# Differential attention's projections: query and value slabs alternate, in place of all queries ahead of all values

## The reference

```python
q, k, v = jnp.split(h @ w_in, 3, axis=-1)                    # latent tokens; the context gives k and v alone
q = rms_norm(q.reshape(b, l, DIFF_HEADS, 2, DIFF_HEAD_DIM), q_gain)
k = rms_norm(k.reshape(b, l, DIFF_HEADS, 2, DIFF_HEAD_DIM), k_gain)
q_l = apply_rope(q_l, cos, sin)
k_l = apply_rope(k_l, cos, sin)
```

## Time and profile before

| | us |
|---|---|
| median of 3 runs | 1271.04 (1270.48 to 1272.4) |
| the profiled execution | 1273.77 |
| its span in the profile | 1272.1 |
| q0 to q7 and the units just behind them, 565 to 613 in the span | 48 |
| the other value units, 613 to 647 | 34 |

### The profile page before, as it was taken

The page is one execution under the profiler, slowest core; times in us unless marked ns, Lnnn a source line. Parts: engine busy times, 40 slices in busy tenths (PEclk is TensorE's granted clock), DMA queues, the critical chain, the costliest instruction groups (busy, mean ns, idle before and its releaser), DMA issues.

```text
span 1272.1 us, 18656 instructions
## 1 busy us (share of the span) xinstructions
PE 1195.5 (94%) x7112; PEld 987.8 (78%) x7112; DVE 703.3 (55%) x1170; ACT 544.3 (43%) x1002; POOL 86.2 (7%) x124
## 2 busy tenths in 40 slices
PE   7999999999999998898978899999989788999998
PEld 4665787787788886677955899999979775798467
DVE  3544567676533334779369554445574635455843
ACT  3234321222232223555258554445465556466742
POOL 0002011122100002000000200000000000020500
PEclk9999999999999999899999999999999999999899
DMA  8889355687522232224320345655534332374011
GB/s 304 315 299 323 130 180 164 196 284 248 189 96 100 100 99 66 66 67 133 100 67 1 100 159 174 194 177 188 160 119 145 100 100 66 61 225 138 33 47 53
DMA packets 121366, 183.32 MB, mean 144 GB/s; under 512 B 4305, under 2 KB 92672, under 8 KB 121296
## 3 DMA queue, kind: packets, MB, share of 16 engines
q1 hardware_dynamic: 113744, 154.64, 36.8%
q0 software_dynamic: 7552, 27.73, 6.9%
HBM read 181.31 MB, written 1.05 MB: 143 GB/s over the span
## 4 chain that ended last, share of the span: by engine, by line
PE 80%; DVE 10%; ACT 4%; issue 3%; POOL 1%; DMA 1%; DVEq 0%; SPq 0%; ACTq 0%; POOLq 0%
PE ps L458 19%; PE ps L459 19%; PE ps L460 19%; PE ps L774 2%; PE ps L775 2%; PE ps L776 2%; PE ps L814 2%; DVE wl L443 1%; PE ps L2038 1%; PE ps L2082 1%; ACT wh L436 1%; DVE big L885 1%; PE ps L2369 1%; PE ps L2371 1%; PE ps L2370 1%
## 5 line engine op out<-in xcount | busy, mean ns | idle before, releaser
L443 DVE TENSOR_TENSOR wl<-raw,wh 128x1024 fp32r<-128x1024 f32 (+1 forms) x246 | 296.4, 1209 | 263.3 <-ACT wh L436 260.7
L458 PE MATMUL ps<-hh,wh 128*128 128x256 f32 (+2 forms) x1256 | 420.3, 335 | 17.9 <-DVE hl L588 11.4
L459 PE MATMUL ps<-hl,wh 128*128 128x256 f32 (+2 forms) x1256 | 411.2, 327 | 0.0
L460 PE MATMUL ps<-hh,wl 128*128 128x256 f32 (+2 forms) x1256 | 410.2, 327 | 0.0
L436 ACT ACTIVATE wh<-raw 128x1024 fp32r<-128x1024 f32 (+1 forms) x246 | 252.8, 1031 | 278.1 <-PE ps L460 256.3
L458 PEld LDWEIGHTS ps<-hh,wh 128*128 128x128 f32 x1256 | 238.8, 190 | 60.6 <-issue 27.5
L460 PEld LDWEIGHTS ps<-hh,wl 128*128 128x128 f32 x1256 | 239.2, 190 | 20.9
L459 PEld LDWEIGHTS ps<-hl,wh 128*128 128x128 f32 x1256 | 238.1, 190 | 22.3 <-issue 1.9
L458 PE MATMUL ps<-ah,wh 128*128 128x256 f32 (+2 forms) x392 | 132.5, 338 | 7.4 <-DVE big L870 3.7
L459 PE MATMUL ps<-al,wh 128*128 128x256 f32 (+2 forms) x392 | 129.7, 331 | 0.0
L460 PE MATMUL ps<-ah,wl 128*128 128x256 f32 (+2 forms) x392 | 129.5, 330 | 0.0
(11 more groups left out here) (225 smaller groups left out, 1427.1 us busy)
## 6 DMA issues: line engine op xcount, KB each, us to landing
raw<-in_ffn_w_in SPq DMA_DIRECT2D x44, 1024.0 KB, 5.1
raw<-in_ffn_w_out SPq DMA_DIRECT2D x22, 1024.0 KB, 5.0
raw<-in_w_in SPq DMA_DIRECT2D x22, 1024.0 KB, 5.3
big<-in_w_ada SPq DMA_DIRECT2D x16, 1024.0 KB, 9.3
big<-in_w_ada POOLq DMA_DIRECT2D x24, 512.0 KB, 4.5
ex<-in_w_ada POOLq DMA_DIRECT2D x24, 512.0 KB, 5.2
raw<-in_diff_w_in SPq DMA_DIRECT2D x12, 1024.0 KB, 5.1
raw<-in_w_out SPq DMA_DIRECT2D x8, 1024.0 KB, 4.9
```

The source lines that it names most:

```text
L443: ins = nc.vector.tensor_tensor(place(wl), v, place(wh).bitcast(F32), ALU.subtract)
L458: nc.tensor.matmul(o, w_hi, m_hi, start=first, stop=False, **kw)
L459: nc.tensor.matmul(o, w_hi, m_lo, start=False, stop=False, **kw)
L460: return nc.tensor.matmul(o, w_lo, m_hi, start=False, stop=last, **kw)
```

## The change

In `slab_starts` the stages `diff_q` and `diff_v` (four slabs each) become one stage `diff_qv` of eight slabs, which alternate: query slab s stands at `DQ_G[s]`, value slab s at `DV_G[s]` behind it. The unit list is built in that order, and SP loads the slabs in it. The list is now k0 to k7, q0 q1, v0 to v3, q2 q3, v4 to v7, q4 q5, v8 to v11, q6 q7, v12 to v15. The number and the size of all instructions and transfers are the same.

```diff
@@ -132,7 +132,7 @@
-              ("diff_k", 4), ("diff_q", 4), ("diff_v", 4), ("diff_out", 4), ("ffn1_in", 22), ("ffn1_out", 11),
+              ("diff_k", 4), ("diff_qv", 8), ("diff_out", 4), ("ffn1_in", 22), ("ffn1_out", 11),
@@ -145,6 +145,8 @@
+DQ_G = [G["diff_qv"] + 2 * s for s in range(4)]
+DV_G = [G["diff_qv"] + 2 * s + 1 for s in range(4)]
@@ -643,13 +645,13 @@
-        for h in range(8):
-            DIFF_UNITS.append(unit("head", 2 * G["diff_q"] + h, KD, 0, P, L, 1,
-                                   red="half", dim=64, gain="dq", rope=("cos_d", "sin_d", L), out=[],
-                                   dst=dq[:, h, :]))
         for s in range(4):
+            for h in (2 * s, 2 * s + 1):
+                DIFF_UNITS.append(unit("head", 2 * DQ_G[s] + h % 2, KD, 0, P, L, 1,
+                                       red="half", dim=64, gain="dq", rope=("cos_d", "sin_d", L), out=[],
+                                       dst=dq[:, h, :]))
             for t in range(4):
-                DIFF_UNITS.append(unit("token", 2 * (G["diff_v"] + s) + 1, KD, 0, 256, P, 2 * (t == 3), tok=t * P,
+                DIFF_UNITS.append(unit("token", 2 * DV_G[s] + 1, KD, 0, 256, P, 2 * (t == 3), tok=t * P,
                                        dst=dv[:, t, s * 256:(s + 1) * 256]))
@@ -1415,9 +1417,9 @@
-            for g, col in ((G["diff_k"], D), (G["diff_q"], 0), (G["diff_v"], 2 * D)):
-                for s in range(4):
-                    load(g + s, d["diff_w_in"][0, :, col + s * 256:col + (s + 1) * 256], KD, 256)
+            for g, col, s in [(G["diff_k"] + s, D, s) for s in range(4)] + \
+                    [(g, col, s) for s in range(4) for g, col in ((DQ_G[s], 0), (DV_G[s], 2 * D))]:
+                load(g, d["diff_w_in"][0, :, col + s * 256:col + (s + 1) * 256], KD, 256)
```

## The result

| | before | after |
|---|---|---|
| median of the runs, us | 1271.52 (6 runs, 1270.48 to 1274.2) | 1266.42 (6 runs, 1264.86 to 1266.65) |
| profiled execution, us | 1273.77 | 1266.24 |
| its span, us | 1272.1 | 1264.5 |

The ratio is 0.9955, with a 95% interval of 0.9942 to 0.9967. So the change makes the kernel faster by 0.45%, which is 5.7 us on the median of before. The forecast was 0.45%, at 1265.3. The measured median is 1.1 us above that, inside the range that was given.

The account below looks back on a forecast made before the run. DVE was taken to bound the query units, PE the value units. With PE waiting for nothing behind v2, the last copy comes 5.67 us earlier: 1271.04 - 5.7 = 1265.3 us, 0.45% less; range 1263.4 to 1267.8.

Parts of the forecast that it names:

- The first units: Behind the keys, v0 to v2 take the places of q2 to q4 and start as those did; nothing gained until v2.
- From v2 to v15: Projection behind v2: PE waits for nothing, 20 units and six sums take 59.44 us; last copy 5.67 us earlier.
- The pace of a matmul: Projection units: the trace's 118 ns per matmul, 2.84 us a unit, stands against the skill's 109 ns, 2.62 us a unit.
- a gain of about 10: Gain if matmuls took 109 ns: the 20 units behind v2 would take 4.4 us less; not adopted.
- The start of the value slabs: At v4, v8, v12 the second half is ready 0.13 us ahead of need; costed at nothing, bound 1.05 us three times.
- the 0.15 from a DVE end to PE's start: Term in the value-slab chain: the split ends at 2.60, plus 0.15 makes the half ready for PE at 2.75.
- The rotations: DVE rotates q0 and q1 under v2 and v3, ending at 586.5; the group's first split can start at 588.5.
- Point 6 of the prediction: Behind the projection: q7's rotations end under v14, ahead of the last copy, so all that follows moves up by the gain.
- The slower rival: Query rotations get in front of the value slabs' splits, each slab 3.1 us late; 1274.6 us, chance 0.03.
- The clock at the start of the attention: Rival: clock falls lie differently over the moved work, up to 1.7 us either side, 1263.6 to 1267.0; chance 0.10.
- Taken back later: Rival: an event of its own time holds the attention or ffn and the gain is lost; 1271 us, chance 0.04.

Follow-up runs that it names:

- the late half: Against the changed kernel, ACT rounds the second half of v4's, v8's and v12's slab twice, so it is ready later; 1268.49 us, ratio 0.9969.

## Why the prediction was right, point by point

- *The first units.* v1 was to start at 577.2 and v2 at 581.4, at the places of q3 and q4. With the 1.56 us by which this execution was ahead, they start at 577.11 and 581.34. The backlog of the keys is worked off once, and the last experiment but one shows that it is the keys': with q0 and q1 moved ahead of k6, waits of 0.46, 0.65 and 1.15 shrink to 0.46 at k6 and 0.46 at v2.
- *From v2 to v15.* Predicted 59.44 + 0.28 = 59.72 us from v2's start to the last copy; measured 639.41 - 579.78 = 59.63. Both terms hold, the 2.84 us of a unit taken from the value stretch and the 0.44 of a sum taken from another part of the kernel. The gain, 5.67 predicted, is 5.85 in the trace. That the ratio of the whole times came out as forecast to the last digit is in part luck: its interval reaches 1.6 us to either side.
- *The pace of a matmul.* The prediction kept the trace's 118 ns against 109, and was right to. The Trainium skill, "TensorE: Matmul & The Clock Gate", section "Back-to-back issue gap", gives the 109 for a matmul by itself and not for a stream in which each has its own weight load, as here (7112 of each). The prediction's "a gain of about 10", worked out from it, is also wrong as a sum: it shortens 20 units of the new order, but 14 of them stand behind v2 in the old order too and would be as much shorter. With both the estimate by that figure is 5.67 + 4.4 - 3.1 = 7.0.
- *The start of the value slabs.* The chain of roundings and splits was right in its order, and cost nothing. Its slack was 0.33 us, not 0.13. The term that was off is the 0.15 from a DVE end to PE's start. With the split delayed, v4 starts within about 0.1 of the split's end (591.03 + 1.22 = 592.25 to 592.32), and its second matmul follows after 0.22, where it takes 0.31 behind a sum. These two, 0.08 and 0.09, are most of the 0.20 by which the count was short.
- *The rotations* end at 585.2 in DVE's rows, and the first split of the group starts at 587.13, 1.9 us later, where I had 2. The scaling of q2 is over at 593.3, ahead of v5's start at 594.8:

```profile
584.78 0.42 DVE L890 TENSOR_TENSOR big<-t,big 128x256 f32<-128x256 f32 x1
...
587.13 1.23 DVE L445 TENSOR_TENSOR wl<-raw,wh 128x1024 fp32r<-128x1024 f32 x1 [1.92 <-ACT wh L438]
...
589.97 2.36 DVE L445 TENSOR_TENSOR wl<-raw,wh 128x1024 fp32r<-128x1024 f32 x2 [1.62 <-ACT wh L438]
...
592.84 0.49 DVE L872 SCALAR_TENSOR_TENSOR nrm<-ps,par,rstd 128x256 f32<-128x256 f32 x1 [0.51 <-ACT rstd L852]
```

- *The end of the rotations.* Point 6 of the prediction had q7's rotation end under v14. It ends at 637.83, under v15, still 1.6 us ahead of the last copy, so it cost nothing.
- *The slower rival* had its decision point at those 2 us. They were there (DVE stood idle for 1.9 us ahead of the first split in the first group, for 2.9 to 3.0 in the later ones), so it did not come near.
- *The clock at the start of the attention.* It fell differently, as that rival allowed, but with little effect. In the changed kernel:

```profile
645.00:650.00 5.00, 4.20 (x12) 1.73 (x12) 3.92 (x10) 2.90 (x10) 0.00 (x0) 0.50 0.54 187
650.00:655.00 5.00, 4.00 (x20) 1.62 (x16) 4.57 (x9) 3.18 (x9) 0.00 (x0) 0.87 0.00 0
```

  In the earlier trace rows it was 0.97 and 0.69, but those stretches begin 2.4 us earlier, counted from the last copy. Over the 20 us behind the last copy the granted clock is 0.91 before and 0.83 after. From the last value copy to the first scaling of the ffn's norm it is 723.74 - 639.41 = 84.33 us against 730.76 - 646.82 = 83.94 before, so the attention took 0.4 longer. The rest of the kernel gave 0.6 back (540.76 against 541.34). Neither is shown to have to do with the change: the changed kernel run again has 0.91 over those 20 us, and takes 722.94 - 639.28 = 83.66.
- *Taken back later:* nothing was. 625.28 us behind the last copy before, 625.09 after.

## What to carry to other kernels

Where two kinds of units pass through the same engines, and one kind loads DVE while the other loads PE alone, the sum of busy times says little: count the longest run of units of the heavy kind, and what backlog DVE brings into it. Units that write banks in turn make PE feel DVE's lateness three units on, so here a pair of heads followed by four units that DVE need not free was enough to hide all of it. Before putting light units there, lay out the preparation of their weights row by row, since slots that are freed in one go leave little slack; here it was a third of a microsecond.

## What the runs showed of the hardware

Eight traces of kernels with the same instructions up to the first key unit have its square at 523.14 to 526.34 us, so a single execution's span can be off by 3 us before the changed code is reached. That is half of the effect of this change, and larger than several of the differences between the experiments. Most of it is there after 23 us: the same copy of DVE starts at 19.61 to 22.51, a spread of 2.90. What remains from that copy to the square is 502.97 to 503.93 us, a spread of 0.96. The shortest is the one trace in which 0.91 of the clock was granted from 500 to 520; the other seven have 0.83 there. So a lower granted clock is not the first thing to suspect when two executions are a few microseconds apart: compare one row early in the trace first. Measured over its own stretch, from one named row to another, each kernel's effect was within 0.3 us of the count, and within 0.6 in the two kernels of the late half and of the query slab between the keys, where a slack or a wait had been mis-sized.
